# An FFN's weight sums moved from GpSimd to DMAs that add into SBUF

## What is computed

```python
def swiglu_ffn(x, w_gate_up, w_down):
    g, u = jnp.split(x @ w_gate_up, 2, axis=-1)
    return (jax.nn.silu(g) * u) @ w_down

for layer in range(2):
    x = x + 0.5 * swiglu_ffn(rms_norm(x, ffn1_norm[layer]), ...)   # 1024 -> 2 x 2816 -> 1024
    x = x + mixer(rms_norm(x, mix_norm[layer]))                    # A, then B
    x = x + 0.5 * swiglu_ffn(rms_norm(x, ffn2_norm[layer]), ...)
return rms_norm(x, final_norm)
```

## Time and profile before

| | |
|---|---|
| median of 3 runs | 2021.71 us (2020.02 to 2022.15) |
| profiled execution | 2022.85 us, its span 2021.1 us |
| mean granted TensorE clock | 0.950 of 2.4 GHz |
| TensorE busy | 1796.9 us (89%), 12889 matmuls |
| VectorE busy | 1664.0 us (82%) |
| GpSimd busy | 1238.7 us (61%) |
| ScalarE busy | 952.1 us (47%) |
| DMA | 172.08 MB in 316675 packets, 311518 of them under 2 KB |

### The profile page before, as it was taken

One profiled execution on the slowest core, in us unless ns is written; L12 is line 12 of the kernel. 1 busy time (PEld: TensorE's weight loads), 2 busy tenths in 40 slices (PEclk: granted clock), 3 DMA queues, 4 the chain that ended last, 5 costly groups with the idle time before them and its releaser, 6 DMA issues. The chain is left out here.

```text
span 2021.1 us, 34518 instructions
## 1 busy us (share of the span) xinstructions
PE 1796.9 (89%) x12889; PEld 1670.4 (83%) x12889; DVE 1664.0 (82%) x2324; ACT 952.1 (47%) x1784; POOL 1238.7 (61%) x863
## 2 busy tenths in 40 slices
PE   4988989999969899899688998999999788898997
PEld 4988979977868898798588988997867588898995
DVE  6799899867678899986778989867796678989997
ACT  4444444546544444444444454444465454444442
POOL 1788798701139978876298788760000178879771
PEclk6999999999989899999898999999999888999999
DMA  3323323343223232333133232334212132332321
GB/s 106 84 84 84 103 77 94 105 115 85 74 63 84 84 105 85 84 105 95 52 84 84 85 103 70 100 90 121 53 40 78 48 95 83 85 86 83 105 74 73
DMA packets 316675, 172.08 MB, mean 85 GB/s; under 512 B 13345, under 2 KB 311518, under 8 KB 316510
## 3 DMA queue, kind: packets, MB, share of 16 engines
q1 hardware_dynamic: 314944, 168.12, 29.6%
q10 hardware_dynamic: 1566, 1.74, 0.3%
HBM read 163.29 MB, written 2.10 MB: 82 GB/s over the span
## 5 line engine op out<-in xcount | busy, mean ns | idle before, releaser
L1767 PE MATMUL bank<-h_all,w_all 128*128 128x256 f32 x2464 | 734.7, 298 | 171.6 <-ACT work L965 95.1
L1768 PE MATMUL bank<-h_all,w_all 128*128 128x256 f32 x2464 | 722.6, 293 | 0.0
L1769 PE MATMUL bank<-h_all,w_all 128*128 128x256 f32 x2464 | 721.8, 293 | 0.0
L1767 PEld LDWEIGHTS bank<-h_all,w_all 128*128 128x128 f32 x2464 | 499.7, 203 | 192.7 <-issue 141.7
L1768 PEld LDWEIGHTS bank<-h_all,w_all 128*128 128x128 f32 x2464 | 500.2, 203 | 0.0
L1769 PEld LDWEIGHTS bank<-h_all,w_all 128*128 128x128 f32 x2464 | 498.9, 202 | 0.0
L1181 DVE TENSOR_TENSOR w_all<-work,w_all 128x1024 fp32r<-128x1024 f32 x360 | 454.3, 1278 | 31.1 <-ACT w_all L865 29.4
L1181 DVE TENSOR_TENSOR w_all<-r_all,w_all 128x512 fp32r<-128x512 f32 (+1 forms) x240 | 349.9, 1458 | 96.7 <-ACT w_all L865 94.8
L723 POOL TENSOR_TENSOR work<-r_all 128x512 f32<-128x512 f32 x120 | 185.8, 1548 | 322.7 <-DMA r_all<-ffn_gu 184.5
L865 ACT ACTIVATE w_all<-work 128x1024 fp32r<-128x1024 f32 x360 | 269.0, 767 | 144.5 <-PE bank L1769 133.9
L1767 PE MATMUL bank<-y_all,w_all 128*128 128x256 f32 x896 | 258.3, 288 | 22.3 <-DVE w_all L1181 17.8
(11 more groups left out here) (186 smaller groups left out, 2865.5 us busy)
## 6 DMA issues: line engine op xcount, KB each, us to landing
r_all<-ffn_gu SPq DMA_DIRECT2D x176, 512.0 KB, 5.2
r_all<-ffn_d SPq DMA_DIRECT2D x70, 512.0 KB, 5.0
r_all<-ffn_d SPq DMA_DIRECT2D x24, 384.0 KB, 3.6
r_all<-a_in SPq DMA_DIRECT2D x10, 512.0 KB, 4.0
r_all<-a_out SPq DMA_DIRECT2D x8, 512.0 KB, 4.3
r_all<-b_out SPq DMA_DIRECT2D x8, 512.0 KB, 3.8
r_all<-b_in SPq DMA_DIRECT2D x5, 512.0 KB, 3.9
r_all<-b_qup SPq DMA_DIRECT2D x16, 144.0 KB, 2.3
```

Source lines behind the costliest of these rows:

```text
L1767: t.matmul(o, wh, xh, start=c == 0 and not on, stop=False, skip_group_check=on)
L1768: t.matmul(o, wh, xl, start=False, stop=False, skip_group_check=on)
L1769: last = t.matmul(o, wl, xh, start=False, stop=c == PAIRED - 1, skip_group_check=on)
```

## The change

The sums are plain sums, made by DMAs that add into SBUF: with signs chosen anew, one chain a21, + a22, + a11, + a12 in place (`chain`, four buffers of 512 columns), and one single sum a21 + a11 (`single`, three buffers). SP loads a21 twice; GpSimd issues the four adding DMAs of each unit (`link` three times, `join` once), each 256 KB from the weights in HBM. Between two links of a chain the sum is read by a fill: `FU` (S1, its buffer in `w_all` alternates), `FB` (S2, now 512 columns), `FD` (S4). The minus signs move to VectorE's mixing of x and to a factor of -0.5. The weights arrive arranged, so that every row of a load is 2 KB or more; SP's loads of a unit are a21, a21, a11 and a12 (512 KB), and a22. The products with `r_x` (`normed_gate`, `normed_silu`) stand in VectorE's order in place of GpSimd's. In ScalarE's and VectorE's order `FB` now precedes `FD`. The buffers of `r_all` are laid out anew, so the first unit's plain load of a stage lies partly over slot 3 of the blocks.

```diff
-P_FILL = {1: FA, 2: FA, 6: FB, 5: FB, 4: FC, 3: FD, 7: FE}
+P_FILL = {1: FA, 2: FA, 6: FB, 5: FU, 4: FC, 3: FD, 7: FE}
...
+            def load_chain(f, u):
+                g = NU * f + u
+                if g >= CHAIN:
+                    sp.wait_ge(fill_lo, fill_count((g - CHAIN) // NU, FD, (g - CHAIN) % NU))
...
+                sp.dma_start(chain[g % CHAIN], unit_source(f, u, A_21)).then_inc(chain_in[g % CHAIN], 16)
+            def load_single(f, u):
...
+                    sp.wait_ge(fill_lo, fill_count((g - SINGLE) // NU, FE, (g - SINGLE) % NU))
+                sp.dma_start(single[u % SINGLE], unit_source(f, u, A_21)).then_inc(single_in[u % SINGLE], 16)
+            def load_plain(f, u):
+                if u >= 3:
+                    sp.wait_ge(fill_lo, fill_count(f, FC, u - 3))
+                elif f > 0:
+                    for i in ((3,), (0, 1), (1, 2))[u]:
+                        sp.wait_ge(split_done, max(n for n in range(SEG_AT[f - 1], SEG_AT[f]) if slot(n) == i) + 1)
+                sp.dma_start(dst[:, 0:2 * S], unit_source(f, u, slice(0, 2 * S))).then_inc(in_, 16)
+                sp.dma_start(dst[:, 2 * S:3 * S], unit_source(f, u, slice(2 * S, 3 * S))).then_inc(in_, 16)
...
-            def weight_sum(f, u, i):
...
-                        g.tensor_tensor(dst, a21, a22, ALU.add).then_inc(sum_done, 1)
...
+            def link(f, u, step):
+                if step == 0:
+                    pool.wait_ge(chain_in[g % CHAIN], 16 * (g // CHAIN + 1))
+                elif step == 1:
+                    pool.wait_ge(fill_lo, fill_count(f, FU, u))
+                else:
+                    pool.wait_ge(fill_lo, fill_count(f, FB, u))
+                part = ((2, 0, 1)[step])
+                pool.dma_start(chain[g % CHAIN], unit_source(f, u, slice(part * S, (part + 1) * S)), accum_op=ALU.add
+                               ).then_inc(chain_sum[g % CHAIN], 16)
+            def join(f, u):
+                pool.wait_ge(single_in[u % SINGLE], single_count(f, u, 1))
+                pool.dma_start(single[u % SINGLE], unit_source(f, u, slice(0, S)), accum_op=ALU.add
+                               ).then_inc(single_sum[u % SINGLE], 16)
...
                 for u in range(NU + 1):
-                    if u < NU:
-                        weight_sum(f, u, 3)
-                    weight_sum(f, u + 1, 0)
-                    weight_sum(f, u + 1, 1)
+                    link(f, u + 1, 1)
+                    link(f, u + 2, 0)
+                    join(f, u + 2)
                     if u == 0:
                         power(m)
...
+                    link(f, u + 1, 2)
...
@@ VectorE, ffn
+                    low_fill(f, FU, u + 1)
...
                     if u > 1 and UNITS[u - 2][0] == "G":
+                        normed_silu(f, u - 2, 1)
                         second_half(f, u - 2)
+                    if gate and u > 0:
+                        normed_gate(f, u, 0, m)
...
                     if u > 0 and UNITS[u - 1][0] == "G":
+                        normed_silu(f, u - 1, 0)
                         first_half(f, u - 1)
...
+                    low_fill(f, FB, u + 1)
+                    if u > 0 and UNITS[u - 1][0] == "G":
+                        normed_gate(f, u - 1, 1, m)
                     low_fill(f, FD, u)
-                    low_fill(f, FB, u + 1)
```

More of the change, by code:

```diff
@@ L108, with silu_order, chain_count, single_count @@
 HALVES = {k: i for i, k in enumerate(half_order())}
+def silu_order():
+    out = []
+    for u in range(1, NU):
+        if u > 1 and UNITS[u - 2][0] == "G":
+            out.append((u - 2, 1))
+        if UNITS[u - 1][0] == "G":
+            out.append((u - 1, 0))
+    return out + [(NU - 2, 1), (NU - 1, 0), (NU - 1, 1)]
+SILU = {k: i for i, k in enumerate(silu_order())}
 def half_count(f, u, half):
     return 2 * TILES * f + HALVES[u, half] + 1
-def sum_count(f, u, i):
-    return 4 * NU * f + 4 * u + i
+CHAIN, SINGLE = 4, 3
+A_21 = slice(3 * S, 4 * S)
+def chain_count(f, u, steps):
+    return 16 * (3 * ((NU * f + u) // CHAIN) + steps)
+def single_count(f, u, steps):
+    return 16 * ((NU * f + u) // SINGLE + steps)
+def unit_count(f, u):
+    return 32 * ((NU * f + u) // 3 + 1)
 def combined():
@@ L181, in loads @@
 def loads():
[L183 to L197, removed]
+    count = [0] * SLOTS
+    block = {}
+    for n in range(len(BLOCKS)):
+        count[slot(n)] += 1
+        block[n] = 16 * count[slot(n)]
+    return block
+BLOCK_LOADS = loads()
 M_A = 4
@@ L348, in build @@
         w_raw = r_all[:, 0:SLOTS, :].rearrange("p s (k m) -> p s k m", m=P)
-        tables = r_all[:, SLOTS:6, :].rearrange("p a b -> p (a b)")[:, 0:3 * S]
+        r_flat = r_all[:, :, :].rearrange("p a b -> p (a b)")
+        tables = r_flat[:, 8 * S:11 * S]
+        plain = [r_flat[:, 3 * i * S:3 * (i + 1) * S] for i in range(3)]
+        single = [r_flat[:, (9 + i) * S:(10 + i) * S] for i in range(SINGLE)]
         def view(at, *shape):
@@ L354, in view @@
             return v.rearrange("p (a b) -> p a b", a=shape[0]) if len(shape) == 2 else v
-        S_2, S_1, S_3, S_4 = range(4)
-        w_sum = view(0, 4, S)
+        chain = [view(i * S, S) for i in range(CHAIN)]
         x_pair = [view(4 * S + i * 2 * S, 4, HN) for i in range(2)]
@@ L489, in build, with product_w, fill, unit_source @@
         block = ctx.enter_context(nc.Block())
-        def product_w(q, c, low):
-            i, j = P_W[q]
+        def product_w(q, u, c, low):
+            i, j = (1 + u % 2, 1) if q == 5 else P_W[q]
             at = j * S + c * P
             return w_all[:, i, low, at:at + P]
[L497 to L511, removed]
-            if kind == FA:
[L513 to L523, removed]
+        def fill(f, kind, u):
+            raw = plain[(u + 2) % 3]
+            linked = chain[(NU * f + u) % CHAIN]
+            if kind == FA:
+                return w_all[:, 0, 0, :], w_all[:, 0, 1, :], raw[:, 0:2 * S]
+            i, j, src = {FC: (2, 0, raw[:, 2 * S:3 * S]), FU: (1 + u % 2, 1, linked), FB: (1, 0, linked),
+                         FD: (3, 1, linked), FE: (3, 0, single[u % SINGLE])}[kind]
+            return w_all[:, i, 0, j * S:(j + 1) * S], w_all[:, i, 1, j * S:(j + 1) * S], src
+        def unit_source(f, u, part):
+            k = UNITS[u]
+            if k[0] == "G":
+                return units_gu[f][k[1], :, part]
+            return units_d[f][PAIRED * k[1] + k[2], :, part]
         def hid_half(t, half):
@@ L582, in load_unit @@
                         sp.wait_ge(mq_ready, 2)
[L583 to L599, removed]
+                if f == 0 and u == 0:
+                    load_plain(f, u)
+                    load_x(2)
+                    load_chain(f, u)
+                    load_x(1)
+                    load_single(f, u)
+                    load_x(3)
+                    return
+                load_chain(f, u)
+                load_single(f, u)
+                load_plain(f, u)
             def load(n, src):
                 f, i = segment(n), n - SEG_AT[segment(n)]
[L603 to L610, removed]
+                if i < SLOTS:
+                    for kind, u in (((FC, NU - 2),), ((FC, NU - 2), (FA, NU - 1)), ((FC, NU - 1),), ((FC, NU - 3),))[i]:
+                        sp.wait_ge(fill_lo, fill_count(f, kind, u))
                 else:
@@ L615, in load, with ffn @@
                 sp.dma_start(dst, src).then_inc(raw_in[slot(n)], 16)
-            def ffn(f, w_gu, w_d, part):
+            def ffn(f, rows, part):
                 for u in range(NU):
-                    load_unit(f, u, w_gu, w_d)
+                    load_unit(f, u)
                     if f == FFNS - 1 and u == 4:
@@ L1178, in low_fill @@
                     return
-                hi, lo, src = fill(kind, u)
+                hi, lo, src = fill(f, kind, u)
                 dve.wait_ge(fill_hi, fill_count(f, kind, u))
@@ L1330, in x_added @@
                 at = xT[:, c, half * HN:(half + 1) * HN]
-                return v.scalar_tensor_tensor(at, src, 0.5, at, ALU.mult, ALU.add)
+                return v.scalar_tensor_tensor(at, src, -0.5 if c < PAIRED else 0.5, at, ALU.mult, ALU.add)
             def hidden_low(f, t):
@@ L1483, in _ @@
             end = SEG_AT[1]
-            n = square(ffn(0, 0), 0.5, G_MIX, end)
+            n = square(ffn(0, 0), -0.5, G_MIX, end)
             def sine_a(c):
```

200 lines of the change are left out of this document (102 added, 98 removed).

## The result

The changed kernel takes 1863.75 us in the median of 4 runs (1858.54 to 1869.23), the kernel before 2020.93 beside it: ratio 0.9222, 95% interval [0.9195, 0.9249]. The profiled execution took 1863.95 us, its span 1862.2, at a mean granted clock of 0.974. Forecast were 1843 and a range of 1800 to 1965. TensorE is busy 1736.1 us of the span (93%), VectorE 1424.5, GpSimd 447.9.

A forecast was written before the change was run, and what follows sets the result against it. GpSimd's queue and VectorE, slowed by its company, were taken to bound the kernel; 2022.85 us less 167.8 in the four stages' counted units and 12 outside them gives 1843 us, range 1800 to 1965.

The forecast's parts named there:

- Where the period came from: GpSimd's 11.7 us of sums and products and VectorE's slowed fills set 11.9 us a unit; TensorE alone wants 10.12.
- mixing units: The 8 of 30 units a stage that also mix a pair: VectorE's 10.5 us plus half a microsecond of waits, 11.0.
- Rival 2: VectorE binds: mixing units cost 12.1 us and others 10.9, 76 us gained in four stages, 1935 us; chance 0.11.
- GpSimd's issues: Four DMA issues a unit in GpSimd's queue at 1.0 to 1.5 us each, 4 to 6 us, hidden behind TensorE.
- rival 4: GpSimd's DMA issues are as slow as its sums were, 2.9 us each: no change; chance 0.03 together with the rest.
- The added row: DMA engine time per row added into SBUF, taken as 163 ns: 5.2 us a unit, 9.0 with plain rows.
- the second sum of the prediction: Alternative DMA total: an added row's two reads in turn cost 192 ns, 6.1 us, together 10.0 us a unit.
- Rival 3: DMA engines saturate: at 259 ns an added row, units take 12.1 us, about 2035 us, slower than before; chance 0.15.
- The links: Three adding DMAs in series per chain: landing taken as 4.5 us each, where 4.6 was the limit.
- the prediction's loop: Chain from one unit's `FU` through link, fills, SiLU to the next: a light and a mixing unit want 2L + 11.0 us.
- rival 1: The link loop binds: at 6 us a link a pair costs 23.0, 107 us gained in four stages, 1904 us; chance 0.14.
- the prediction's signs of being wrong: An added packet over 200 ns, ScalarE waiting for a link in most units, or GpSimd's queue running behind.

The follow-up runs named there:

- a_products: The kernel before with only the four normed products per gate unit moved to VectorE, the sums left on GpSimd: 2012.81 us, 0.9951 of the kernel before.
- c_nosingle: The changed kernel without the single sum: one load and one of four adding DMAs a unit dropped, product 7 lacks a21: 1833.99 us.
- k_vector: The changed kernel with the single sum made by VectorE in place of a load and an adding DMA: 1869.8 us.
- f_early: The changed kernel with fill `FU` one unit sooner, so link 1 is issued some 3 us earlier: 1862.52 us.
- kf_ring: The changed kernel with the single sum on VectorE, 1536 bytes of descriptor room and fill `FU` a unit earlier: 1862.4 us.
- k_ring: The changed kernel with the single sum on VectorE and 1536 in place of 1024 bytes of descriptor room per partition: 1865.41 us.
- e_ring1536: The changed kernel with 1536 in place of 1024 bytes of descriptor room per partition, warm-up matmuls reading another buffer: 1852.6 us.
- d_more: The changed kernel with 66 more plain loads of 256 KB, 22 in each of stages 1 to 3, that nothing reads: 1916.69 us.
- e_ring512: The changed kernel with 512 in place of 1024 bytes of descriptor room per partition: 2753.39 us.
- j_sum: The changed kernel with the single sum made by GpSimd itself in place of a load and an adding DMA: 1901.84 us.

## Why the prediction was right, and where it was off

**Where the period came from: right.** GpSimd's queue of 11.7 us and VectorE's company set 11.9 us; with both gone the quiet units take 10.08 us, where 10.12 was read for TensorE alone. `a_products` shows the other half of the diagnosis: products off GpSimd without the sums off it leave VectorE in company and gain 10 us. The prediction never priced the halves apart; a subtraction for each would not have given 10, 0 and 157. It also left the clock out, because its quiet stretch had 1.00. Over the counted units of the four stages TensorE's busy time fell from 1225.9 to 1167.7 us for some 9500 matmuls either way, at a granted clock of 0.94 to 0.96 before and 0.98 to 0.99 after. So 58 of the 145.9 us gained there are TensorE's own, some 46 of them by the ratio of the mean clocks (an estimate: 1167.7 x (0.982/0.945 - 1)), and the 1.8 us lost in each unit were not all waiting. The low clock followed waits: TensorE was busy 16.3 of the 20 us from 640, and the next 20 us had 0.83. The sum took no harm, since the new units were priced from a stretch at full clock.

**VectorE: right in sum, not in place.** Fills run at 0.69 and 1.22 us. The mixing units were taken at 11.0 us; most take 11.9 to 13, and the units after them 8.2 to 9.6. A pair of the two is 21.4 us in the mean, forecast 21.2. Timeline of VectorE after, over such a pair:
```profile
641.56 1.22 DVE L1187 TENSOR_TENSOR w_all<-r_all,w_all 128x1024 fp32r<-128x1024 f32 x1
...
647.08 0.69 DVE L1187 TENSOR_TENSOR w_all<-work,w_all 128x512 fp32r<-128x512 f32 x1 [0.37 <-ACT w_all L868]
...
649.81 0.42 DVE L1457 TENSOR_TENSOR work<-bank,work 128x256 f32<-128x256 f32 x1 [1.10 <-ACT work L991]
...
653.95 1.21 DVE L1187 TENSOR_TENSOR w_all<-r_all,w_all 128x1024 fp32r<-128x1024 f32 x1
...
663.19 1.22 DVE L1187 TENSOR_TENSOR w_all<-r_all,w_all 128x1024 fp32r<-128x1024 f32 x1
```
12.39 us less two waits is 10.9 of VectorE's own, forecast 10.5. The wait of 1.10 us for ScalarE's copy `u_3` stands in every mixing unit of the 28 pairs, in `c_nosingle` and `k_vector` too; half a microsecond was put for all waits, and they are 1.5 in the mean. Rival 2 (1935 us) had 12.1 for a mixing unit, which is near, and 10.9 for the others, which take 10.1 or, after a mixing unit, 9.1; so it fell. That VectorE has no spare time in the mixing units is what `k_vector` measured.

**GpSimd's issues: right, and one wait not thought of.** 0.93 to 0.98 us was forecast as 1.0 to 1.5, and rival 4 fell. The room for descriptors stood nowhere in the prediction. It is worth 11 us. Second units of stages 2 to 4 were priced at 10.2 and take 13.9, 14.5 and 13.7, 11.5 us over; with more room they take 11.3 to 12.3, so 6.7 us of the 11.5 were room and 4.8 were not.

**The added row: the mis-sized term.** The step took 163 ns "nearest to a transfer that touches SBUF on both sides"; measured are 192. A unit's DMA time is 512 x 192/16 = 6.1 us where 5.2 stood, with 0.367 x 10.6 = 3.9 of loads (forecast 3.8) 10.0 us in place of 9.0: the second sum of the prediction, level with TensorE and without margin. The DMA share of the counted units is 0.92 to 0.96, forecast 0.80 to 0.95. The rule cited there from the Trainium skill ("Collectives: The Full Stack", on why ReduceScatter is half of AllGather), that two source reads halve the rate, agrees with 192 against 96 ns. Rival 3 needed 252 ns to make the kernel slower; it fell, but its threshold of 196 ns, where TensorE stops being the bound, was missed by 4.

**The links: the size was wrong and the consequence too.** Links land in 5.8 us where 4.5 was taken and 4.6 was the limit. By the prediction's loop a pair would be 2 x 5.8 + 11.0 = 22.6 us; it is 21.4, and issuing link 1 some 3 us earlier gains nothing (`f_early`, and `kf_ring` against `k_ring`). In `k_vector` links land in 4.4 us and the pair is longer, 22.1. So rival 1's loop does not close as written. One of the prediction's signs of being wrong came all the same: ScalarE waits for a link 118 times in 120 units. It was no sign of a kernel outside the forecast's range. ScalarE's 314.6 us of waits for links are mostly harmless: `c_nosingle` has the same two waits at 217.1 us with TensorE at 98.35 of 100. Which link, if any, still costs in the mixing units stays open.

**The sum.** Stages gained 37.6, 36.5, 35.6 and 36.2 us, together 145.9 for 167.8 forecast. Outside the counted units 158.9 - 145.9 = 13.0 came for 12. The shortfall of 21.9 us is the 11.5 of the second units and about 10 spread over the others; which wait each of these came from was not taken apart. `c_nosingle`, relieved of most of both, is at 1834, 9 under the forecast: the forecast is about what the kernel takes when the DMA engines have a margin, as the 9.0 us supposed; `c_nosingle` has 0.77 to 0.79 of share in the stages. The best complete kernel is `e_ring1536`, 1852.6 us.

## What to carry to other kernels

When two engines hold each other up, price a change as a whole and test its halves: here one half alone gave 10 us, the other nothing, and both 157. Work moved to DMAs costs the DMA engines time as on any engine; add up each unit's rows by their kind, and where the sum comes within a few per cent of the bound, expect each further load to cost its full price, as in `d_more`. A queue that issues DMAs should hold no product that others wait for, and it needs room for as many descriptors as are to be in flight.

## What the runs showed of the hardware

- A 2 KB row that a DMA adds into SBUF costs one of the 16 DMA engines 192 to 194 ns in the changed kernel and 190 to 200 in the others, a plain one from HBM 96. An adding DMA of 256 KB holds GpSimd for 0.9 us and lands 3.8 us after its issue when little overlaps (`e_ring512`), 5.8 at a DMA share of 0.97.
- The room for descriptors is a resource of its own: 512, 1024 and 1536 bytes per partition gave 2753, 1864 and 1853 us. Where it lacks, the profile shows idle time before a DMA of GpSimd that ends in "issue".
- A GpSimd addition of 1.64 us, begun 0.16 us after a VectorE fill that lasts 1.22 us when free, made that fill last 2.88 us (`j_sum`).
- TensorE's mean granted clock, of 2.4 GHz, was 0.94 to 0.96 in the stages of before, where it was busy 89 to 90% of the time, and 0.98 to 0.99 after, at 95 to 97%. Some 9500 matmuls took 58 us less of busy time.
